# A hybrid decoder step with expert retrieval: the front computed for 2, 3 and 3 blocks in place of 1, 3 and 4, a seventh row buffer, and a table that places the steps

## The reference, cut to what matters

```python
# the front: per position, dense
mod = silu(c) @ w_ada + b_ada                      # sh1, sc1, gt1, sh2, sc2, gt2
z = (rmsnorm(x, g_mix) * (1 + sc1) + sh1) @ w_in   # a_lin, a_gate, u, v, g_a, g_b
a = a_lin * sigmoid(a_gate)                        # branch A: causal depthwise conv, width 31
a = silu(layernorm(causal_dwconv(concat(hist, a)), g_cn, b_cn)) @ w_conv_out
b_br = (u * chunk_spatial_gate(layernorm(v))) @ w_gmlp_out     # branch B
x = x + gt1 * ((sigmoid(g_a) * a + sigmoid(g_b) * b_br) @ w_out)
n2 = rmsnorm(x, g_ffn) * (1 + sc2) + sh2
# routing: 8 heads, best 16 of 128 keys twice, best 16 of their 256 sums
q = n2 @ w_q; sc1, i1 = top_k(q1 @ k1, 16); sc2, i2 = top_k(q2 @ k2, 16)
top, pos = top_k(sc1 + sc2, 16); eid = i1 * 128 + i2 at pos; g = softmax(top)
# the retrieval: 128 experts for each position, each a row of u_tab and one of v_tab
act = gelu(einsum("tnd,td->tn", u_tab[eid], n2))
x = x + gt2 * einsum("tn,tnd->td", g * act, v_tab[eid])
y = rmsnorm(x, g_final)
```

## Time and profile before

| | us |
|---|---|
| median of 3 runs | 3511.39 (3509.34 to 3520.03) |
| the profiled execution | 3523.17 |
| its span in the trace | 3521.6 |
| first gather issued | 273.9 |
| busy: PE, DVE, POOL, ACT | 2047.3, 2446.7, 1230.9, 440.0 |
| moved by DMA | 1232.08 MB, mean 350 GB/s |

### The profile page before, as it was taken

One profiled execution on the slowest core, in us unless ns is written; L12 is line 12 of the kernel. 1 busy time (PEld: TensorE's weight loads), 2 busy tenths in 40 slices (PEclk: granted clock), 3 DMA queues, 4 the chain that ended last, 5 costly groups with the idle time before them and its releaser, 6 DMA issues. The chain is left out here.

```text
span 3521.6 us, 28830 instructions
## 1 busy us (share of the span) xinstructions
PE 2047.3 (58%) x9548; PEld 993.7 (28%) x9548; DVE 2446.7 (69%) x6290; ACT 440.0 (12%) x1031; POOL 1230.9 (35%) x1046
## 2 busy tenths in 40 slices
PE   6873878987267767688678733333333333355333
PEld 4762534544044445355345400000000000000000
DVE  1447575479898887655768997787868678556665
ACT  1121101011111201110211010011010101010200
POOL 0001211222223433234444433444444444434433
PEclk9886979998579879799789855555555555555555
DMA  7744756698669999899999977999999999998998
GB/s 298 303 158 155 298 208 259 265 353 316 244 259 356 384 309 369 333 370 419 416 403 407 381 291 320 421 422 421 419 421 422 421 415 402 419 404 347 422 423 342
DMA packets 183925, 1232.08 MB, mean 350 GB/s; under 512 B 30512, under 2 KB 31152, under 8 KB 36320
## 3 DMA queue, kind: packets, MB, share of 16 engines
q0 software_dynamic: 148608, 1082.20, 76.4%
q1 hardware_dynamic: 35168, 148.05, 10.8%
HBM read 1221.14 MB, written 9.02 MB: 349 GB/s over the span
## 5 line engine op out<-in xcount | busy, mean ns | idle before, releaser
L1047 POOL DMA_INDIRECT big<-in_experts,eid x920 | 1096.4, 1192 | 2071.1 <-PE ps L767 1613.0
L1509 DVE SCALAR_TENSOR_TENSOR big<-big,xr 128x1024 f32<-128x1024 f32 x920 | 1113.7, 1224 | 504.1 <-DMA big<-in_experts,eid 498.8
L767 PE MATMUL ps<-big,wd 128*32 128x512 f32 x3680 | 724.0, 871 | 1067.0 <-DVE wd L1526 1065.0
L532 PE MATMUL ps<-big,wring 128*128 128x260 f32 (+2 forms) x2400 | 646.4, 423 | 81.4 <-issue 56.2
L532 PEld LDWEIGHTS ps<-big,wring 128*128 128x128 f32 x2400 | 447.6, 201 | 320.7 <-issue 170.9
L767 PEld LDWEIGHTS ps<-big,wd 128*32 128x32 f32 x3680 | 84.9, 127 | 1569.2 <-DVE wd L1526 1523.6
L989 ACT ACTIVATE gel<-act 128x2 f32<-128x2 f32 x516 | 104.8, 203 | 2535.0 <-DVE big L1509 2295.6
L1526 DVE TENSOR_SCALAR wd<-mask,gel,gate 128x32 f32<-128x32 f32 x1024 | 277.9, 363 | 154.1 <-ACT gel L989 143.5
L767 PE MATMUL ps<-w,wd 128*32 128x512 f32 x208 | 100.3, 1061 | 166.4 <-DVE wd L1526 162.5
L1207 DVE SCALAR_TENSOR_TENSOR arena<-arena,wdw 128x128 f32<-128x128 f32 (+2 forms) x360 | 182.6, 565 | 0.0
L684 PE MATMUL ps<-wring,mbuf 128*128 128x256 f32 (+1 forms) x528 | 125.8, 394 | 11.4 <-DMA wring<-in_w_out 6.5
(11 more groups left out here) (219 smaller groups left out, 1873.7 us busy)
## 6 DMA issues: line engine op xcount, KB each, us to landing
wring<-in_w_in SPq DMA_DIRECT2D x40, 1024.0 KB, 10.2
wring<-in_w_q SPq DMA_DIRECT2D x19, 1024.0 KB, 9.1
big<-in_experts,eid POOLq DMA_INDIRECT x920, 11.8
wring<-in_w_ada SPq DMA_DIRECT2D x12, 1024.0 KB, 7.4
wring<-in_w_out SPq DMA_DIRECT2D x9, 1024.0 KB, 9.7
big<-in_w_ada SPq DMA_DIRECT2D x6, 1024.0 KB, 7.2
xr<-in_w_ada SPq DMA_DIRECT2D x6, 1024.0 KB, 8.8
big<-in_w_in SPq DMA_DIRECT2D x4, 1024.0 KB, 14.7
```

Source lines behind the costliest of these rows:

```text
L532: mm = mmul(out, piece(n)[:, c, col:col + P], src[:, c, gi * tg:(gi + 1) * tg], start=(c == 0), stop=(c == k - 1))
L767: mm = mmul(ps[QUAD * j:QUAD * (j + 1), half, :], wd[:, 2 * (at % 4) + jj, :], row(2 * slot + jj)[:, D + 512 * h:D + 512 * (h + 1)], start ...
L1047: gp.indirect_dma_start(row(r), None, t["experts"], bass.IndirectOffsetOnAxis(ap=index, axis=0)).then_inc(s_row[r], 16)
L1509: last = v.scalar_tensor_tensor(out=row(r)[:, 0:D], in0=row(r)[:, 0:D], scalar=1.0, in1=x, op0=ALU.mult, op1=ALU.mult, accum_out=act[:, c: ...
```

## The change

- The groups are blocks 0 and 1 (256 columns), blocks 2 to 4 (384 columns), and blocks 5 to 7 with the samples (392 columns in one run, `ng` 1). Layouts of the shared memory follow from the groups.
- Row buffers are planned singly. There are 7 up to `WIDE_AT`, which is now pair 320, and 10 from there.
- ACT writes `gelu(mask * dot)` straight into the two weight tiles, with the dot as its scale (two 128x32 instructions in place of one 128x2); DVE then multiplies both with their gates in one 128x64 instruction. The wait for the tile's last reader moves from DVE to ACT.
- Steps and route pieces are placed by estimated loads. `front_loads` gives each step a pair of numbers, for PE and for DVE, in us; `ROUTE_LOADS` gives each route piece's on DVE. `place_steps` gives every pair a room of the pace less 1.6 on PE and less 3.0 on DVE, and fills it in order. The pace is raised from 5.2 by 0.05 until all fits. G2's steps go to pairs 0 to 123, after the 10 route pieces of block 1; G3's to pairs 128 to 311, after the 20 route pieces of blocks 3 and 4. The pieces of the last group's later blocks stand 3 pairs apart from pair 320 on.
- SP loads `x` of both blocks of G1 at the start. PE's norm stage stands one step later.

```diff
-NB1 = 4
-GW = 520
+STARTS = [0, 2, 5]
+NB1 = STARTS[-1]
...
+ROWS_1, ROWS_2 = 7, 10
...
-ROUTE_STEP = 4
...
-HEAVY = 3
-END_B = 60
-END_C = 4 * PAIRS - 8
-WIDE_AT = 4 * PAIRS
+WIDE_AT = NB1 * PAIRS
+PE_BASE, DVE_BASE = 1.6, 3.0
+ROUTE_LOADS = [1.6, 1.6, 3.9, 3.6, 5.5, 5.5, 5.5, 8.4, 0.7, 3.5]
...
     for at in range(NPAIRS):
-        free = range(3 if at < WIDE_AT else 5)
-        slot = min(free, key=lambda i: -1 if newest[i] is None else newest[i])
...
+        tiles = []
+        for _ in range(2):
+            free = range(ROWS_1 if at < WIDE_AT else ROWS_2)
+            r = min(free, key=lambda i: -1 if newest[i] is None else newest[i])
...
-        G1 = group(1, [0], P, xn1[:, 0:1, :], mbuf)
-        G2 = group(2, [1, 2, 3], 3 * P, xn1[:, 1:4, :], mbuf)
-        G3 = group(3, list(range(NB1, NBT)), 260, xn2, wring)
+        for n in range(1, LAST):
+            blocks = list(range(STARTS[n - 1], STARTS[n]))
+            GROUPS.append(group(n, blocks, len(blocks) * P, ...))
+        GROUPS.append(group(LAST, list(range(NB1, NBT)), GT // -(-GT // 512), xn2, wring))
...
+        def front_loads(g):
+            tg, ng, nb = g.tg, g.ng, g.nb
+            mm, op, tap = 4 * max(0.4, 0.0021 * tg), 0.15 + 0.0007 * tg, (0.3 + 0.0012 * g.np) * taps_per_step[g.n]
+            light = (0.1, 0.1)
+            head = [*norm_loads(g), *[light] * 5, *[(mm, op / 4)] * (4 * CC * ng), *[light] * 5]
+            steps = head + [(mm, tap)] * (2 * CC * ng) + [light] * 5
...
+        def place_steps(loads, head, pieces, lo, hi, pace):
+            pe_room, dve_room = pace - PE_BASE, pace - DVE_BASE
+            pe, dve, at, done, out = 0.0, 0.0, 0, 0, {}
+            for pair_ in range(lo, hi):
+                pe, dve = min(pe + pe_room, 2 * pe_room), min(dve + dve_room, 2 * dve_room)
+                first, limit = at, len(loads) if done == len(pieces) else head - 8
+                piece = done < len(pieces) and dve > 0
+                if piece:
+                    dve -= pieces[done]
+                    done += 1
+                while at < limit and pe > 0 and dve > 0:
+                    pe, dve, at = pe - loads[at][0], dve - loads[at][1], at + 1
+                out[pair_] = (at - first, piece)
+            return out if at == len(loads) and done == len(pieces) else None
...
+            for g in GROUPS[1:]:
+                lo, hi = PAIRS * STARTS[g.n - 2], PAIRS * STARTS[g.n - 1] - (4 if g.n < LAST else 8)
...
+                found, pace = None, 5.2
+                while found is None:
+                    pace += 0.05
+                    found = place_steps(loads, head, routes, lo, hi, pace)
...
+            each = (SAMPLE_AT - 8 - WIDE_AT) // rest
+            pieces += [WIDE_AT + each * i for i in range(rest)]
...
             def gelu(at):
                 c = 2 * (at % 4)
+                if at >= 4:
+                    act_.wait_ge(S["rows_used"], at - 3)
                 act_.wait_ge(S["dots"], at + 1)
-                ac(gel[:, c:c + 2], act[:, c:c + 2], ACT.Gelu).then_inc(S["gelu"], 1)
...
+                    for jj in range(2):
+                        last = ac(wd[:, c + jj, :], mask[:], ACT.Gelu, scale=act[:, c + jj:c + jj + 1])
...
                 for jj in range(2):
+                    r, _, earlier = PLAN[at][jj]
+                    if earlier is not None:
+                        pool.wait_ge(S["rows_used"], earlier + 1)
...
                 dve.wait_ge(S["gelu"], at + 1)
-                if at >= 4:
-                    dve.wait_ge(S["rows_used"], at - 3)
...
-                        last = v.tensor_scalar(wd[:, c, :], mask[:], gel[:, c:c + 1],
-                                               gate[:, b % 4, 2 * half + jj, m:m + 1], ALU.mult, ALU.mult)
+                    last = v.tensor_tensor(wd[:, c:c + 2, :], wd[:, c:c + 2, :],
+                                           gate[:, b % 4, 2 * half:2 * half + 2, m:m + 1].broadcast_to([P, 2, QUAD]), ALU.mult)
```

More of the change, by code:

```diff
@@ L355, in spread_front @@
-        def spread_front():
[L357 to L364, removed]
-                        at += 1
-                    steps[pair_] = (g.n, at - first)
-            return steps
@@ new lines, in later_turns @@
+        def later_turns(g):
+            return [(g, turn) for turn in range(1, g.nb)]
+        def spread_front():
+            steps, pieces = [(None, 0)] * NPAIRS, []
+            for g in GROUPS[1:]:
+                lo, hi = PAIRS * STARTS[g.n - 2], PAIRS * STARTS[g.n - 1] - (4 if g.n < LAST else 8)
+                loads, head = front_loads(g)
+                routes = ROUTE_LOADS * len(later_turns(before[g.n]))
+                found, pace = None, 5.2
+                while found is None:
+                    pace += 0.05
+                    found = place_steps(loads, head, routes, lo, hi, pace)
+                for at, (count, piece) in found.items():
+                    steps[at] = (g.n, count)
+                    pieces += [at] if piece else []
+            rest = ROUTE_PIECES * (GL.nb - 1) + 1
+            each = (SAMPLE_AT - 8 - WIDE_AT) // rest
+            pieces += [WIDE_AT + each * i for i in range(rest)]
+            return steps, pieces
@@ L443, in _ @@
                 if n == 16:
[L444 to L453 removed]
+                    bring_x(GROUPS[1])
@@ new lines, in _ @@
+            for g in GROUPS[1:-1]:
+                for n in range(first_piece[g.n], first_piece[g.n + 1] + (3 if g.n == LAST - 1 else 0)):
+                    if n == first_piece[g.n] + 4 and g.n < LAST - 1:
+                        bring_x(GROUPS[g.n])
+                    with_spill(n, g)
+            ahead = before[LAST]
+            sp.wait_ge(*ahead.to("oa_mm", KC * ahead.ng))
+            sp.wait_ge(*ahead.to("s_done", NCH))
+            sp.wait_ge(*ahead.to("sq_act", 1))
+            sp.wait_ge(*ahead.to("tables", 1))
@@ L748, in value @@
                 b, half, m = place(at)
-                slot = PLAN[at][0]
+                rows = [row(tile[0]) for tile in PLAN[at]]
                 pe.wait_ge(S["weights"], at + 1)
@@ L788, in begin @@
                         made[0] += 1
-            beside_peer(begin, value, {2: front(G2), 3: front(G3)}, lambda at: None, share=0.5)
+            beside_peer(begin, value, {g.n: front(g) for g in GROUPS[1:]}, lambda at: None, share=0.5)
         @block.scalar
@@ L1019, in extra @@
                     root(1, 0, NB)
-            beside_peer(gelu, lambda at: None, {2: front(G2), 3: front(G3)}, extra)
+            beside_peer(gelu, lambda at: None, {g.n: front(g) for g in GROUPS[1:]}, extra)
             square(NB)
@@ L1620, in _ @@
             dve.wait_ge(S["mask_made"], 1)
-            beside_peer(dots, weigh, {2: front(G2), 3: front(G3)}, extra)
+            beside_peer(dots, weigh, {g.n: front(g) for g in GROUPS[1:]}, extra)
             take_acc(2 * NB)
```

322 lines of the change are left out of this document (171 added, 151 removed).

## The result

The changed kernel takes 3480.97 us (median of 6 runs, 3476.01 to 3494.57) against 3511.03 for the kernel before (6 runs): ratio 0.9918, 95% interval 0.9901 to 0.9936. It is faster, by 30 us where 189 were forecast, and lies above the range given (3430). The profiled execution took 3482.56 us, its span is 3480.8.

What follows compares the result with a forecast made beforehand. DMA bounds from 2171 us on; before that no engine is full and a short ring starves. 431 + 781 + 1049 + 1070 = 3331 us of span, 3333 with 1.6 around it, scaled to a median of 3322; range 3235 to 3430.

Steps and rivals of the forecast that it cites:

- Step 1: Start to pair 0's dots: G1 with two blocks is longer and fully exposed, +126, ending at 431 us.
- Steps 4 and 5: Pairs 312 to the end: 1070 us; masked gelu: costs nothing, covered by DMA.
- Steps 2 and 3: Pairs 0 to 127 beside G2's front: 781 us; pairs 128 to 311 beside G3's front: 1049 us.
- what a short ring loses: Pairs beside a front: an added loss from few buffers, 0.3 us a pair to pair 127, then 0.25.
- the pace of 5.8: Pairs 0 to 127: us a pair by the rows' durations, where the table's search ends at 6.85.
- the bytes' 5.45: Pairs 128 to 311: us a pair for 421 MB in 1000 us, above the pace by rows of 5.2.
- With a seventh buffer there is half a pair, 2.5 us, more to ride out a late step: Pairs 0 to 127: the extra buffer's slack, a reason to take the ring's loss as 0.3 us a pair.
- 30-us lumps: Ends of the old fronts: 36 and 32 us with one pair's value instructions and leftover steps; claimed to be gone.
- A: The 312 pairs beside fronts: the ring still starves, 7.0 us a pair, median some 3674, slower; chance 0.07.
- C: The 312 pairs go at the table's paces, 6.85 and 6.10: median 3490; weaker form 3409; chance of either 0.15.
- B: Stretches with a front: PE's clock falls to 0.50, median 3613, slower; chance 0.03.
- D: Whole run: DMA's 421 GB/s is reached throughout, 719 and 1000 us beside the fronts, median 3196; chance 0.08.

Runs made afterwards that it cites:

- x3: The changed kernel with the gelu and the weights made as before (one 128x2 gelu, two DVE instructions): 3482.58 us, ratio 0.9912.
- x1: The changed kernel with 6 single row buffers up to pair 320 in place of 7: 3564.02 us, ratio 1.0143.
- x10: The changed kernel with x2's piece order, x6's split routes, x7's loads, and 6 row buffers up to pair 320 in place of 7: 3486.78 us, ratio 0.9921.
- x2: The changed kernel with weight pieces loaded in another order, each to the ring place that comes free first: 3440.41 us, ratio 0.9788.
- x13: The changed kernel with the last group's 392 columns in two runs of 196: 3463.05 us, ratio 0.9857.
- x14: The changed kernel with x2's order, x6's split routes, x7's loads, and the last group in two runs of 196 columns: 3398.72 us, ratio 0.9675.
- x15: x14 with the second group's 384 columns as two runs of 192 as well: 3385.01 us, ratio 0.9636.
- x4: The changed kernel with the front's steps spread by the old weights of 1 to 3 over the same pairs: 3504.28 us, ratio 0.9984.
- x5: The changed kernel with the groups of before and 6 row buffers, leaving the table and the masked gelu: 3525.1 us, ratio 1.0035.
- x11: x10 with the groups of before, so 6 row buffers as well: 3458.09 us, ratio 0.9847.
- x7: x2 with the table's loads and rooms set to what the trace has: 3422.81 us, ratio 0.9745.
- x6: x2 with each block's routing cut into 15 pieces where it had 10: 3404.03 us, ratio 0.9689.
- x8: The kernel before, with x2's piece order and nothing else: 3473.04 us, ratio 0.9873.

## Why the prediction was wrong, point by point

**Step 1 (G1, 431 us) was right**: 427.3; L605 took 188.6 us for 183, the first gather went out at 395.6.

**Steps 4 and 5 were right**: 1071.3 for 1070, and nothing for the gelu (x3).

**Steps 2 and 3 failed in the term "what a short ring loses"**, 0.3 and 0.25 us a pair on top of the larger of pace and bytes. Work and bytes were right to 7%; a pair took 6.70 and 6.11 us, so in the prediction's own sum the term came out as 0.9 on top of the pace of 5.8, and as 0.66 on top of the bytes' 5.45. That left 352 GB/s before pair 128, under the 360 that the prediction named as breaking it. The term's form was wrong, not only its size: it is a loss at every round, on which the number of buffers, the order of the weight pieces, the placing and the step length each act, as the runs show. I had started from the 0.5 of the old last group, with steps of 260 columns, as the price for any front, and it is the cheapest front in the trace: the wait for PE is 1.0 us there (pairs 128 to 239) and 8.4 beside the old front of 384 columns, packed into pairs 0 to 59.

- "With a seventh buffer there is half a pair, 2.5 us, more to ride out a late step" was wrong in kind. It shortens the round by taking the first gather out of it, and is worth 75 to 79 us with or without long steps (x1, x10). Without it the change loses 50 us (x1), which the prediction had nowhere.
- The fronts of 384 and 392 columns make the weights wait for PE 3 to 6 us. The four stops of 14 us for weight pieces are worth 41 to 46 us of time (x2), the last group's step length 11 to 21 (x13, x14) and the second's another 14 (x15). The stops stood in the trace before as well, and I read the waits of that stretch only down to its longest.
- Placement: the "30-us lumps" did go, and the table is worth 23 us in the new groups (x4), but with gelu it costs 12 in the old ones (x5). I had priced the lumps by what one lasts, without a view of what else the placing does.
- Regrouping itself, at equal buffers, loses 26 to 38 us (x5, x11). The prediction counted 126 us ahead of the pairs (121 measured between x5 and x1) and what pairs 0 to 127 get back (173). For pairs 128 to 311, 64 of which get a front that they didn't have, it forecast 21 us less than before, and between x5 and x1 they lose 95.

From the kernel before by x5 and x1 to the kernel after, the steps are +12 us (table and gelu), +38 (groups) and -79 (buffer), -29 by ratio. That they add up says nothing, since each is the difference of neighbours; and in another order the steps have other sizes, as the table shows (+12 with gelu at x5, -23 at x4).

**The rivals.** *A* was nearest in mechanism (front steps delay the return of a buffer), and not in size: 1982 us for the 312 pairs is 6.35 each, under the 6.5 from which it ends slower. *C* had nearly the time (1999 for the 312) for a wrong reason, as x7 shows. *B*: the clock fell only to 0.79 and 0.75, from 0.82 to 0.86; PE's busy time was 20 and 46 us over forecast, of which this is a part. The rows agree with the Trainium skill's page TensorE: Matmul & The Clock Gate, Part 1, where activity releases the throttle: in pairs 128 to 143, with PE busy 36 of 107 us, the grant is 0.52. *D*: 352 and 374 GB/s, not 421; x15 comes to 372 and 389.

**What stays open**: x15 takes 1897 us for the 312 pairs, 67 more than the forecast's 1830 and 178 more than the bytes' 1719. Which part of the round holds them, what in x6 gave 36 us, and why the weights wait longer for PE with the table (x5), the runs don't tell. An eighth buffer, which would bring the second gather out of the three-pair round, and a fourth place for weight pieces weren't tried; whether memory has room for either no run shows.

## What to carry to other kernels

Where gathers run in a ring of few buffers, find the round first: pair each fetch with its use and its release, and see where it spends its time. Round over depth comes near the measured time of any full ring, also where DMA is the limit (5.1 against 5.17 us in the tail), so it doesn't name the limit, and busy shares and bytes are only lower bounds. A wait on an engine that is a third idle can cost time, but not all of what is cut there comes back: 1.1 us less wait for PE gave 0.3 us of a round here (x13). So try each part with a run. And look at each ring's order of release: a piece that is held longer than its neighbours empties a ring in strict rotation, and a few lines of order were worth more here than the whole new schedule (x8).

## What was not expected of the hardware

- Matmuls at 196 columns cost no more in sum than half as many at 392: 307.4 against 307.6 us of PE, while the time in weight loads went from 159 to 281 us beside them (x13).
- An ACTIVATE of 32 columns with its scale from memory took 321 ns where one of 2 columns with a constant scale took 203 and one of 128 took 277: above both bounds that I had put. The Trainium skill, ScalarE: Activation LUTs, section What ACT_TABLE_LOAD costs, has some 93 ns for a pointer operand; by its figures the estimate is 186 + 27 + 93 = 306 ns, near the 321, and with its overlap of 93 ns two take 0.52 us, where the trace has 0.53.
- A weight piece issued into gathers was used 14 us later, with DMA at 425 GB/s in between; three pieces of 1 MB went out together there, where the median landing of such pieces in the kernel before was 8 to 10 us by its profile's page.
